# Two of four memory-value products moved to the experts' norm block, one behind a post norm's sums, with a reordered branches block, in an fp32 transformer kernel

## Chip, cores and metric

One NeuronCore of one Trainium2 chip runs the whole forward pass in one launch. The metric is the device time of one execution in microseconds (us), median of the runs shown. The profile is of one execution, whose span is counted from its first to its last instruction.

## What is computed

Three residual blocks over 256 tokens of width 1024, in fp32: feed-forward and gating layers, an attention block with a mixture of 32 experts, and a third block, which is the one that the change touches. Its part that matters here, cut:

```python
h = rms_norm_3(x, norm_mix_pre[l])
proj = h @ w_in[l]
q, k, v, u, gate_logits = jnp.split(proj, splits, axis=-1)
gate_attn, gate_ssm = jnp.split(jax.nn.sigmoid(gate_logits + b_gate[l]), 2, axis=-1)
o_attn = stick_breaking_attention(q, k, v)
o_ssm = s5_branch(u, ...)
merged = gate_attn * (o_attn @ w_branch_attn[l]) + gate_ssm * (o_ssm @ w_branch_ssm[l])
x = x + rms_norm_3(merged @ w_out[l], norm_mix_post[l])
h = rms_norm_3(x, norm_xa_pre[l])
mem_n = rms_norm_3(mem, norm_mem[l])
xa = memory_cross_attention(h, mem_n, xa_wq[l], xa_wk[l], xa_wv[l], xa_wo[l])
```

`memory_cross_attention` begins with `k = mem_n @ wk` and `v = mem_n @ wv`, both 256 x 1024 by 1024 x 1024. They depend on `mem` and weights alone, so they can be multiplied at any time before the cross attention. `s5_branch` ends with `y = gelu(y)` and `y * sigmoid(y @ w_glu + b_glu)`.

## The kernel before

The program is a row of blocks (`nc.Block`); in each, the five engines run their own streams, and all meet at its end, so that none begins the next block before the last is done. Within a block the order on an engine is the order of the code, and semaphores tie the engines. Weights pass through a ring of eight 1 MB slots in SBUF (`Ring`); a unit of weights is one slot, loaded by SyncE's queue once the slot's last reader is done. PSUM has eight banks, each with a full and a free semaphore (`Banks`).

The experts' stage (`run_items`) goes through (expert, token group) items. Each item uses slots 0 to 7 and four more for its expert's weights. Beside the items, `MemoryRows` normalizes and turns `mem` into the tile `memory`, done by item 17. After the last item comes the experts' norm block, `rmsnorm` (L320): ScalarE squares the expert sum, VectorE adds the squares, TensorE sums them over partitions with ones (L357), ScalarE takes the root (L346), VectorE inverts it (L374), scales (L382) and adds to the residual (L386). SyncE loads six units for the next block in it.

`two_branches` then runs `dense_up` (its first unit is L1089) for q, k, v and u, and after it the branches block, `branches` (L3642 on). In that block TensorE interleaves three things:

- the stick-breaking attention: scores (L3724), turned weights (L3737) and values (L3749). The logarithms and exponentials between them are ScalarE's (L3819 to L3826) and the suffix sums VectorE's (L3920 to L3924);
- the state-space scan in four steps: inputs (L3759), copies by ScalarE (L3858), the scan and its products by VectorE (L3941 to L3958), outputs (L3770), then skip sums (L3962), a gelu (L3888) and the GLU product (L3804);
- twenty "native" units (`Native`, `native.multiply`, L1118) that fill the gaps: four of keys, four of values, eight of gates and four of the attention branch. Keys are copied by ScalarE at L3837, values at L3842, gates pass a sigmoid (L3849), and branch units are gated by VectorE (L3973). They use three slots (unit n loads once unit n-3 is multiplied) and two banks in turn (unit n waits until unit n-2 is read).

SyncE's stream in this block is all twenty unit loads first, and then the load of the GLU weights (L3702), which only needs the attention values to be done. ScalarE copies the first keys after `log_fail(3)`, and the third key unit needs that bank.

Behind it come `dense_down` blocks: the state-space branch, the output projection with `PostNorm` (squares L654, sums L644 and L647, root L656, scaling L675, addition L681), the cross query (first unit L820), the cross attention, its projection, and the convolutional feed-forward. Each takes its slots from the ring in turn.

## Time and profile before

| | us |
|---|---|
| median of 3 runs (lowest, highest) | 2831.14 (2826.31, 2832.01) |
| the profiled execution's own time | 2825.68 |
| its span | 2823.9 |
| TensorE (PE) busy | 2648.1, 94% of the span |
| VectorE (DVE) busy | 1431.8, 51% |
| ScalarE (ACT) busy | 968.0, 34% |
| mean granted TensorE clock, of full speed | 0.967 |

The span's shares are averages over stages with different limits. The stage of the change lies between 2229 us (the norm block) and 2530 us (the block after the post norm). The trace records a fp32 matmul as two rows, so that a native unit of 16 matmuls (keys, values and gates) shows as x32, and a branch unit of 8 as x16. A row "PEq" as the releaser of an idle time is the meeting of the engines at a block's end. The clock column is the granted clock as a share of 2.4 GHz: 0.50 is 1.2 GHz.

### The profile page before, as it was taken

What the parts mean: (1) busy time and instruction counts of PE and PEld (TensorE: products, weight loads), DVE (VectorE), ACT (ScalarE), POOL (GpSimd) and SP (SyncE); (2) the same over time, 40 slices, a digit from 0 to 9 for tenths busy, and PEclk for the clock granted to TensorE, in tenths of its full rate; (3) what the DMA queues carried; (4) which work ended last, traced back from release to release, by engine and by line L of the source; (5) the groups of instructions that cost most, each with busy time, mean ns of one, the idle gap of its engine ahead of it and who ended that gap; (6) DMA issues with size and microseconds to landing.
All of it is one profiled execution on the core that took longest, in us unless ns stands there. A gap on an engine that the chain in (4) does not pass through costs nothing. (4 is left out here: it accounts for less than half of the span.)

```text
span 2823.9 us, 41236 instructions
## 1 busy us (share of the span) xinstructions
PE 2648.1 (94%) x16344; PEld 1958.3 (69%) x16345; DVE 1431.8 (51%) x1975; ACT 968.0 (34%) x1179; POOL 7.8 (0%) x15
## 2 busy tenths in 40 slices
PE   7999899999999989799999999999999789988998
PEld 6898788988998977654444444444444378777988
DVE  6846468577468647533244222222212457255893
ACT  4425446355346422421111211211212262123662
POOL 0000000000000000000000000000000000000000
PEclk9999999999999999889999999999999899999999
DMA  7664546657465631189979999999989534442452
GB/s 231 233 225 153 209 140 202 232 169 256 169 217 181 221 137 60 53 336 420 420 308 420 419 420 419 420 421 420 421 345 401 206 96 121 136 158 90 149 193 75
DMA packets 259034, 698.81 MB, mean 247 GB/s; under 512 B 18403, under 2 KB 177838, under 8 KB 209614
## 3 DMA queue, kind: packets, MB, share of 16 engines
q1 hardware_dynamic: 258452, 695.89, 64.8%
q8 instruction: 82, 1.34, 0.2%
q10 hardware_dynamic: 474, 1.37, 0.2%
q14 instruction: 26, 0.21, 0.0%
HBM read 696.16 MB, written 1.05 MB: 247 GB/s over the span
## 5 line engine op out<-in xcount | busy, mean ns | idle before, releaser
L854 DVE TENSOR_TENSOR weight_parts<-weight_slots,weight_parts 128x2048 fp32r<-128x2048 f32 x208 | 473.7, 2288 | 181.3 <-ACT weight_parts L848 179.4
L3093 PE MATMUL bank<-weight_slots,item_x 128*64 128x512 f32 x2176 | 495.8, 604 | 23.5 <-DMA weight_slots<-in_w_mlp 23.5
L848 ACT ACTIVATE weight_parts<-weight_slots 128x2048 fp32r<-128x2048 f32 x208 | 393.4, 1908 | 215.6 <-DMA weight_slots<-in_ffn_w_out 79.8
L1061 PE MATMUL bank<-h_parts,weight_parts 128*128 128x512 f32 x1536 | 384.1, 392 | 0.0
L3093 PEld LDWEIGHTS bank<-weight_slots,item_x 128*64 128x64 f32 x2176 | 151.8, 138 | 315.3 <-issue 287.7
L3268 DVE TENSOR_TENSOR expert_sum_then_keys<-bank,expert_sum_then_keys 128x512 f32<-128x512 f32 x136 | 84.5, 683 | 496.2 <-PE bank L3137 496.2
L866 PE MATMUL bank<-hidden_high,weight_parts 128*128 (+1 forms) x1760 | 314.5, 281 | 8.5 <-DVE weight_parts L854 8.5
L1061 PEld LDWEIGHTS bank<-h_parts,weight_parts 128*128 128x128 f32 x1536 | 275.0, 188 | 47.9
L866 PEld LDWEIGHTS bank<-hidden_high,weight_parts 128*128 128x128 f32 x1760 | 271.0, 189 | 9.5 <-issue 9.5
L3124 PE MATMUL bank<-weight_slots,item_act 128*64 128x512 f32 x1088 | 246.3, 606 | 6.6 <-DVE item_act L3261 3.2
L866 PE MATMUL bank<-hidden_low,weight_parts 128*128 (+1 forms) x880 | 246.6, 280 | 0.0
L1063 PEld LDWEIGHTS bank<-h_parts,weight_parts 128*128 128x128 f32 x1536 | 205.9, 188 | 15.9
L1063 PE MATMUL bank<-h_parts,weight_parts 128*128 128x256 f32 x1536 | 209.6, 278 | 0.0
L3124 PEld LDWEIGHTS bank<-weight_slots,item_act 128*64 128x64 f32 x1088 | 80.1, 141 | 171.0 <-issue 170.2
L3188 ACT ACTIVATE item_hidden<-bank 128x512 f32<-128x512 f32 x68 | 36.9, 595 | 431.0 <-PE bank L3093 431.0
L866 PEld LDWEIGHTS bank<-hidden_low,weight_parts 128*128 128x128 f32 x880 | 165.9, 189 | 0.0
L3080 PEld LDWEIGHTS bank<-item_select,tokens_then_values 128*128 128x128 f32 x1088 | 130.3, 196 | 29.7 <-issue 26.8
L3080 PE MATMUL bank<-item_select,tokens_then_values 128*128 128x64 f32 x1088 | 135.6, 279 | 2.5 <-DVE item_select L3235 2.5
L3202 ACT ACTIVATE item_y<-bank 128x512 f32<-128x512 f32 x34 | 20.3, 597 | 325.8 <-PE bank L3124 325.8
L3253 DVE TENSOR_TENSOR item_glu<-bank,b_columns 128x512 f32<-128x512 f32 x34 | 23.5, 692 | 206.2 <-PE bank L3106 206.2
L866 PE MATMUL bank<-h_parts,weight_parts 128*128 128x256 f32 x1008 | 120.6, 280 | 3.6 <-DVE weight_parts L854 3.6
L1409 ACT ACTIVATE low_sums<-bank 128x512 f32<-128x512 f32 x88 | 52.5, 597 | 206.4 <-PE bank L1063 206.4
(591 smaller groups left out, 3251.8 us busy)
## 6 DMA issues: line engine op xcount, KB each, us to landing
weight_slots<-in_w_mlp SPq DMA_DIRECT2D x384, 1024.0 KB, 17.4
weight_slots<-in_ffn_w_in SPq DMA_DIRECT2D x88, 1024.0 KB, 5.1
weight_slots<-in_ffn_w_out SPq DMA_DIRECT2D x44, 1024.0 KB, 7.3
weight_slots<-in_ffn_w_up SPq DMA_DIRECT2D x22, 1024.0 KB, 5.2
weight_slots<-in_a_w_in SPq DMA_DIRECT2D x16, 1024.0 KB, 6.8
weight_slots<-in_w_in SPq DMA_DIRECT2D x16, 1024.0 KB, 5.7
weight_slots<-in_ffn_w_down SPq DMA_DIRECT2D x11, 1024.0 KB, 7.2
weight_slots<-in_a_w_out SPq DMA_DIRECT2D x8, 1024.0 KB, 13.3
```

Source lines behind the costliest of these rows:

```text
L848: K.nc.scalar.activation(high, source, ACT.Copy).then_inc(K.high_written.sem, 1)
L854: K.nc.vector.tensor_tensor(low, place, high.bitcast(F32), ALU.subtract)\
L866: m = K.nc.tensor.matmul(out, stationary[a], moving[b], start=start and n == 0, stop=stop and n == 2, **flags)
L1061: K.nc.tensor.matmul(ps, high[k], flat(pair[:, k, :, :]), start=k == 0, stop=False, skip_group_check=True)
L1063: last = K.nc.tensor.matmul(ps[:, 0:S], low[k], pair[:, k, 0, :], start=False, stop=k == DT - 1, skip_group_check=True)
L1409: K.nc.scalar.activation(self.lows[:, b, g, :, :], K.banks.columns(ats, 1), ACT.Copy).then_inc(K.lows_copied.sem, 1)
L3080: m = nc.tensor.matmul(ps[(2, 7)[q]][:, t % 4 * CAP:(t % 4 + 1) * CAP], M.tokens[:, b, t * P:(t + 1) * P], sel[:, b, :], start=b == 0, sto ...
L3093: m = nc.tensor.matmul(ps[c // 2][half(c % 2), :], x[:, s, :], ring.slot(s)[:, c * 512:(c + 1) * 512], start=s == 0, stop=s == 7, skip_gro ...
L3124: m = nc.tensor.matmul(ps[3][half(c), :], act_t[:, turned_tile(t), :], ring.slot(s)[:, kk * D + c * 512:kk * D + (c + 1) * 512], start=t = ...
L3188: m = nc.scalar.activation(hid[:, b, :], ps[b][:, :], copy)
L3253: link(v.tensor_tensor(glu[:, :, :], ps[4][:, :].rearrange("p (t s) -> p t s", t=DT), bias(0), ALU.add))
L3268: v.tensor_tensor(part, ps[4 + j][:, :], part, ALU.add).then_inc(sem.added, 1)
```

## The change

Of the four value units, two (`late_values`, banks 4 and 5, ring slots 6 and 7) are loaded at the end of the experts' stage, behind SyncE's wait for the last item's use of their slot, and multiplied in the experts' norm block: the first half of unit 0 ahead of the sum matmuls, its second half and unit 1 behind them, and ScalarE's two copies behind the root. One (`value`, bank 4, the next ring slot) is loaded behind the output projection's weights and multiplied behind the post norm's sums, with its copy behind the root. The fourth stays a native unit. For this the tile `memory` lives until the post norm, and the first gates get a buffer of their own. All ring units taken after it move on by one slot.

In the branches block there are seventeen native units. SyncE loads units 0 to 7, then the GLU weights, then the rest. ScalarE copies the first keys ahead of `log_fail(3)`. One branch unit comes ahead of the last state outputs and is gated ahead of the skip sums, so between the last state outputs and the GLU product stands one branch unit where there were two gate and two branch units.

```diff
@@ -317,7 +317,7 @@
-def rmsnorm(K, src, dst, gain, tiles, shift=None, add_to=None, loads=None, modulation=None, room=None):
+def rmsnorm(K, src, dst, gain, tiles, shift=None, add_to=None, loads=None, modulation=None, room=None, beside=()):
@@ -347,10 +349,14 @@
                 modulation.read_rows(act)
+            for unit in beside:
+                unit.read(act)
...
+            for unit in beside[0:1]:
+                unit.multiply(pe, (0,))
             K.banks.vacant(pe, bank)
@@ -358,6 +364,8 @@
                 modulation.turn(pe)
+            for n, unit in enumerate(beside):
+                unit.multiply(pe, (0, 1) if n else (1,))
@@ -646,6 +654,8 @@
         m.then_inc(K.banks.full[6], 1)
+        if self.beside is not None:
+            self.beside.multiply(pe, (0, 1))
@@ -655,6 +665,8 @@
             .then_inc(K.banks.free[6], 1)
+        if self.beside is not None:
+            self.beside.read(act)
@@ -2980,8 +2992,9 @@
-        run_items(K, a, M, T, memory)
-        rmsnorm(K, M.sum[:, :, :], None, lambda t: K.gate2[:, t:t + 1], DT, add_to=K.x[:, :, :], loads=following.issue)
+        run_items(K, a, M, T, memory, values)
+        rmsnorm(K, M.sum[:, :, :], None, lambda t: K.gate2[:, t:t + 1], DT, add_to=K.x[:, :, :], loads=following.issue,
+                beside=values)
@@ -3070,6 +3083,10 @@
                     sp.dma_start(ring.slot(s), w2[bass.ds(e, 1), s - 8].rearrange("e p n -> p (e n)")).then_inc(loaded[s], 16)
+            n = number_of(sp)
+            for unit in values:
+                sp.wait_ge(used[unit.unit[0]], n)
+                unit.issue(sp)
@@ -3499,17 +3516,63 @@
+class MemoryValues:
+    def __init__(self, K, weights, mem, out, bank):
+        self.K, self.weights, self.mem, self.out, self.bank = K, weights, mem, out, bank
+        self.unit = K.ring.take()
+    def plan(self):
+        self.at = self.K.banks.take(self.bank)
+        self.K.ring.freed_by(self.unit[0], self.K.banks.full[self.bank], self.at[2] + 1)
+    def issue(self, sp):
+        K = self.K
+        K.ring.vacant(sp, self.unit)
+        sp.dma_start(K.ring.slot(self.unit[0]).rearrange("p (t n) -> p t n", n=256),
+                     self.weights.rearrange("(t p) n -> p t n", p=P)).then_inc(K.ring.loaded[self.unit[0]], 16)
+    def multiply(self, pe, blocks):
+        K, b = self.K, self.at[0]
+        slot = K.ring.slot(self.unit[0])
+        for block in blocks:
+            if block == 0:
+                K.banks.vacant(pe, self.at)
+                K.ring.arrived(pe, self.unit)
+            for k in range(DT):
+                m = K.nc.tensor.matmul(K.ps[b][:, block * 256:(block + 1) * 256], self.mem[:, k, block * P:(block + 1) * P],
+                                       slot[:, k * 256:(k + 1) * 256], start=k == 0, stop=k == DT - 1)
+            if block == 1:
+                m.then_inc(K.banks.full[b], 1)
+    def read(self, act):
+        K, b = self.K, self.at[0]
+        K.banks.ready(act, self.at)
+        K.nc.scalar.activation(self.out, K.ps[b][:, :].rearrange("p (b n) -> p b n", b=TB), ACT.Copy).then_inc(K.banks.free[b], 1)
+class Together:
+    def __init__(self, *parts):
+        self.parts = parts
+    def issue(self, sp):
+        for part in self.parts:
+            part.issue(sp)
...
-    def __init__(self, K, a, stack):
+    def __init__(self, K, a, stack, turned_rows):
...
-        self.K = K
+        self.K, self.turned_rows = K, turned_rows
...
-        self.turned_rows = stack.enter_context(nc.sbuf_tensor("memory", [P, DT, S], F32))
@@ -3597,14 +3660,16 @@
-        o = buffer("attention_out", 4, S)
-        gates = [memory.turned_rows[:, :, :], early[:, 4 * S:12 * S].rearrange("p (t s) -> p t s", s=S)]
+        o, first_gates = buffer("attention_out", 4, S), buffer("first_gates", DT, S)
+        gates = [first_gates[:, :, :], early[:, 4 * S:12 * S].rearrange("p (t s) -> p t s", s=S)]
...
-        dense_down(K, y, w_ssm, Gated(K, K.h, gates[1]), w_out)
-    return w_out
+        value = MemoryValues(K, a["xa_wv_3"][0][:, 2 * 256:3 * 256], memory.turned_rows, v_mem[:, :, 2 * 256:3 * 256], 4)
+        value.plan()
+        dense_down(K, y, w_ssm, Gated(K, K.h, gates[1]), Together(w_out, value))
+    return w_out, value
@@ -3683,7 +3748,7 @@
-    value_at = [native.add(a["xa_wv_3"][0][:, j * 256:(j + 1) * 256], mem, DT, True) for j in range(4)]
+    value_at = native.add(a["xa_wv_3"][0][:, 3 * 256:4 * 256], mem, DT, True)
@@ -3695,11 +3760,12 @@
         def _(sp):
-            native.load(sp)
+            native.load(sp, 0, 8)
             for at in turned_at[1]:
...
             sp.dma_start(glu, a["ssm_w_glu_3"][0].rearrange("(t p) n -> p t n", p=P)).then_inc(glu_loaded, 16)
+            native.load(sp, 8, len(native.units))
             w_ssm.issue(sp)
@@ -3792,8 +3858,7 @@
-            for n in range(14, 18):
-                native.multiply(pe, n)
+            native.multiply(pe, 14)
@@ -3804,8 +3869,8 @@
                 m.then_inc(banks.full[at[0]], 1)
-            native.multiply(pe, 18)
-            native.multiply(pe, 19)
+            native.multiply(pe, 15)
+            native.multiply(pe, 16)
@@ -3836,11 +3901,10 @@
-            def memory_values(j):
-                at = value_at[j]
-                banks.ready(act, at)
-                nc.scalar.activation(v_mem[:, :, j * 256:(j + 1) * 256], ps[at[0]][:, :].rearrange("p (b n) -> p b n", b=TB),
...
+            def memory_values():
+                banks.ready(act, value_at)
+                nc.scalar.activation(v_mem[:, :, 3 * 256:4 * 256], ps[value_at[0]][:, :].rearrange("p (b n) -> p b n", b=TB),
@@ -3863,8 +3927,8 @@
             exponentials(1)
+            keys(0)
             log_fail(3)
-            keys(0)
             exponentials(2)
@@ -3873,16 +3937,16 @@
-            memory_values(0)
-            memory_values(1)
+            memory_values()
+            gate(0)
...
-            memory_values(2)
-            memory_values(3)
+            gate(1)
+            gate(2)
...
-            gate(0)
-            gate(1)
+            gate(3)
+            gate(4)
...
-            for j in range(2, 8):
+            for j in range(5, 8):
@@ -3922,6 +3986,13 @@
+            def branch(j):
+                at = branch_at[j]
+                banks.ready(dve, at)
+                banks.read(dve, gate_at[j])
+                V.tensor_tensor(flat(K.h[:, 2 * j:2 * j + 2, :]), ps[at[0]][:, :], flat(gates[0][:, 2 * j:2 * j + 2, :]), ALU.mult)\
+                    .then_inc(banks.free[at[0]], 1)
@@ -3956,6 +4027,7 @@
                 V.tensor_tensor(im_cos, wim, c, ALU.mult).then_inc(products_written, 1)
+            branch(0)
             for n in range(Q):
@@ -3966,14 +4038,7 @@
-            def branch(j):
-                at = branch_at[j]
-                banks.ready(dve, at)
-                banks.read(dve, gate_at[j])
-                V.tensor_tensor(flat(K.h[:, 2 * j:2 * j + 2, :]), ps[at[0]][:, :], flat(gates[0][:, 2 * j:2 * j + 2, :]), ALU.mult)\
-                    .then_inc(banks.free[at[0]], 1)
-            for j in range(4):
+            for j in range(1, 4):
@@ -4146,14 +4211,17 @@
-            nc.sbuf_tensor("tokens_then_values", [P, TB, D], F32) as values:
+            nc.sbuf_tensor("tokens_then_values", [P, TB, D], F32) as values, nc.sbuf_tensor("memory", [P, DT, S], F32) as mem:
...
-            T, memory = S5Operands(K, a, stack), MemoryRows(K, a, stack)
+            T, memory = S5Operands(K, a, stack), MemoryRows(K, a, stack, mem)
+            K.ring.next, K.ring.limit = 6, SLOTS
+            late_values = [MemoryValues(K, a["xa_wv_3"][0][:, j * 256:(j + 1) * 256], mem, values[:, :, j * 256:(j + 1) * 256], 4 + j)
+                           for j in range(2)]
...
-            experts(K, a, T, memory, keys, values, branch_weights)
-            mixed_weights = two_branches(K, a, T, memory, keys, values, branch_weights)
-        up_weights = cross_attention(K, a, mixed_weights, keys, values, lambda: PairWeights(K, a["ffn_w_up_3"][0]))
+            experts(K, a, T, memory, keys, values, branch_weights, late_values)
+            mixed_weights, value = two_branches(K, a, T, memory, keys, values, branch_weights)
+        up_weights = cross_attention(K, a, mixed_weights, value, keys, values, lambda: PairWeights(K, a["ffn_w_up_3"][0]))
```

TensorE at the end of the experts' stage and in the norm block, before; the tile names are those of the sums of squares and the experts' weights:

```order
L3124 MATMUL bank<-weight_slots,item_act 64x512 x16
L3137 MATMUL bank<-item_gates_t,item_y 128x256 x8
L3043 UNCONDITIONAL_BRANCH
L351 UNCONDITIONAL_BRANCH
L357 MATMUL bank<-norm_squares,consts 128x256 x2
L330 UNCONDITIONAL_BRANCH
L956 UNCONDITIONAL_BRANCH
L1089 MATMUL bank<-h_normed,weight_slots 128x256 x8
```

and with the change:

```order
L3141 MATMUL bank<-weight_slots,item_act 64x512 x16
L3154 MATMUL bank<-item_gates_t,item_y 128x256 x8
L3056 UNCONDITIONAL_BRANCH
L355 UNCONDITIONAL_BRANCH
L3544 MATMUL bank<-weight_slots,memory 128x256 x8
L363 MATMUL bank<-norm_squares,consts 128x256 x2
L3544 MATMUL bank<-weight_slots,memory 128x256 x24
L332 UNCONDITIONAL_BRANCH
L968 UNCONDITIONAL_BRANCH
L1101 MATMUL bank<-h_normed,weight_slots 128x256 x8
```

L3544 is the value product; its first 8 matmuls stand ahead of the 2 sum matmuls, and 24 between those and the end of the block.

TensorE at the end of the branches block, before (L3770 state outputs, L3804 the GLU product, `attention_out` the branch units):

```order
L3759 MATMUL bank<-s_u,s_b 128x256 x8
L1118 MATMUL bank<-h_normed,weight_slots 128x256 x32
L3770 MATMUL bank<-weight_slots,s_c 32x256 x16
L1118 MATMUL bank<-h_normed,weight_slots 128x256 x32
L3770 MATMUL bank<-weight_slots,s_c 32x256 x16
L1118 MATMUL bank<-h_normed,weight_slots 128x256 x32
L1118 MATMUL bank<-attention_out,weight_slots 128x256 x16
L3804 MATMUL bank<-qkv_then_gates,spare 128x256 x16
L1118 MATMUL bank<-attention_out,weight_slots 128x256 x16
L3694 UNCONDITIONAL_BRANCH
```

and with the change (L3836 state outputs, L3869 the GLU product):

```order
L3825 MATMUL bank<-s_u,s_b 128x256 x8
L1130 MATMUL bank<-h_normed,weight_slots 128x256 x32
L3836 MATMUL bank<-weight_slots,s_c 32x256 x16
L1130 MATMUL bank<-h_normed,weight_slots 128x256 x16
L1130 MATMUL bank<-attention_out,weight_slots 128x256 x8
L3836 MATMUL bank<-weight_slots,s_c 32x256 x16
L1130 MATMUL bank<-attention_out,weight_slots 128x256 x8
L3869 MATMUL bank<-qkv_then_gates,spare 128x256 x16
L1130 MATMUL bank<-attention_out,weight_slots 128x256 x16
L3759 UNCONDITIONAL_BRANCH
```

Three units fewer stand in the block, 8 branch matmuls stand ahead of the last state outputs, and 8 between them and the GLU product in place of 48.

SyncE in the branches block, before:

```order
L3696 UNCONDITIONAL_BRANCH
L3631 DMA weight_slots<-in_xa_wk 128x8x256 x4
L3631 DMA weight_slots<-in_xa_wv 128x8x256 x4
L3631 DMA weight_slots<-in_w_in 128x8x256 x8
L3631 DMA weight_slots<-in_w_branch_attn 128x4x256 x4
L3702 DMA spare<-in_ssm_w_glu 128x4x512
L712 DMA weight_slots<-in_w_branch_ssm 128x2x1024 x2
L3694 UNCONDITIONAL_BRANCH
```

and with the change:

```order
L3761 UNCONDITIONAL_BRANCH
L3696 DMA weight_slots<-in_xa_wk 128x8x256 x4
L3696 DMA weight_slots<-in_xa_wv 128x8x256
L3696 DMA weight_slots<-in_w_in 128x8x256 x3
L3767 DMA spare<-in_ssm_w_glu 128x4x512
L3696 DMA weight_slots<-in_w_in 128x8x256 x5
L3696 DMA weight_slots<-in_w_branch_attn 128x4x256 x4
L724 DMA weight_slots<-in_w_branch_ssm 128x2x1024 x2
L3759 UNCONDITIONAL_BRANCH
```

The load into `spare` (the GLU weights) has moved ahead of five gate loads and all branch loads.

## Rows read from the trace of the kernel before

**Rows 1.** Page, part 1: busy time, share of the span, instructions.

```profile
PE 2648.1 (94%) x16344; PEld 1958.3 (69%) x16345; DVE 1431.8 (51%) x1975; ACT 968.0 (34%) x1179; POOL 7.8 (0%) x15
```

**Rows 2.** Timeline across the experts' end, the norm block and the next block's start (start us, us, engine, line).

```profile
2229.58 2.19 ACT L344 ACTIVATE norm_squares<-expert_sum_then_keys 128x512 f32<-128x512 f32 x4 [4.37 <-PEq L3043]
...
2233.05 2.05 PE L357 MATMUL bank<-norm_squares,consts 128*128 128x256 f32 x4 [5.79 <-DVE norm_squares L367]
...
2240.72 2.29 DVE L386 TENSOR_TENSOR x_residual<-x_residual,norm_squares 128x2048 f32<-128x2048 f32 x1
2243.29 2.19 ACT L488 ACTIVATE qkv_then_gates<-x_residual 128x512 f32<-128x512 f32 x4 [7.68 <-PEq L330]
...
2244.08 5.35 PE L1089 MATMUL bank<-h_normed,weight_slots 128*128 128x256 f32 x16 [8.98 <-DVE h_normed L494]
```

**Rows 3.** Windows: us, busy of PE, PEld, DVE, ACT, POOL, granted clock, DMA.

```profile
2227.30:2230.00 2.70, 0.00 (x0) 0.00 (x0) 1.63 (x3) 0.42 (x1) 0.00 (x0) 1.00 0.00 0
2230.00:2233.00 3.00, 0.00 (x0) 0.00 (x0) 2.08 (x3) 2.98 (x5) 0.00 (x0) 0.56 0.59 147
...
2301.00:2304.00 3.00, 2.86 (x9) 2.42 (x10) 1.81 (x4) 2.97 (x4) 0.00 (x0) 0.68 1.10 349
2519.30:2523.00 3.70, 3.67 (x9) 2.98 (x10) 3.63 (x10) 3.70 (x5) 0.00 (x0) 0.50 0.82 313
```

**Rows 4.** TensorE's timeline, the branches block from its first key on.

```profile
2301.14 15.74 PE L1118 MATMUL bank<-memory,weight_slots 128*128 128x256 f32 x64 [2.25 <-DMA weight_slots<-in_xa_wk]
...
2320.46 7.17 PE L1118 MATMUL bank<-memory,weight_slots 128*128 128x256 f32 x32 [2.71 <-ACT expert_sum_then_keys L3837]
...
2341.32 14.08 PE L1118 MATMUL bank<-weight_slots,memory 128*128 128x256 f32 x64
...
2420.20 1.93 PE L3770 MATMUL bank<-weight_slots,s_c 128*32 128x256 f32 x32
...
2446.43 10.03 PE L3804 MATMUL bank<-qkv_then_gates,spare 128*128 128x256 f32 x32 [3.38 <-DMA spare<-in_ssm_w_glu]
2456.29 7.07 PE L1118 MATMUL bank<-attention_out,weight_slots 128*128 128x256 f32 x32
2465.85 8.83 PE L820 MATMUL bank<-qkv_then_gates,weight_slots 128*128 128x256 f32 x32 [2.49 <-PEq L3694]
```

**Rows 5.** ScalarE's timeline in the branches block.

```profile
2315.33 1.04 ACT L3819 ACTIVATE weight_slots<-weight_slots 128x1024 f32<-128x1024 f32 x1
...
2319.83 0.58 ACT L3837 ACTIVATE expert_sum_then_keys<-bank 128x512 f32<-128x512 f32 x1
...
2437.03 1.28 ACT L3888 ACT_TABLE_LOAD   x1
2438.33 1.06 ACT L3888 ACTIVATE qkv_then_gates<-qkv_then_gates 128x1024 f32<-128x1024 f32 x1
```

**Rows 6.** VectorE's timeline: the state chain's first and last instruction, the skip sums.

```profile
2343.83 1.22 DVE L3941 TENSOR_TENSOR weight_slots<-weight_slots,s_angle 128x1024 f32<-128x1024 f32 x1 [3.68 <-ACT weight_slots L3859]
...
2411.59 1.22 DVE L3958 TENSOR_TENSOR weight_slots<-weight_slots 128x1024 f32<-128x1024 f32 x1
...
2422.20 0.87 DVE L3962 SCALAR_TENSOR_TENSOR qkv_then_gates<-s_u,params,bank 128x256 f32<-128x256 f32 x2 [8.61 <-PE bank L3770]
```

**Rows 7.** SyncE's timeline: the transfer of the GLU weights.

```profile
2440.18 0.37 SPq L3702 DMA_DIRECT2D spare<-in_ssm_w_glu  x1
```

**Rows 8.** Page, part 6: one weight transfer of 1 MB (last figure: us to landing).

```profile
weight_slots<-in_ffn_w_up SPq DMA_DIRECT2D x22, 1024.0 KB, 5.2
```

**Rows 9.** Timelines of TensorE and VectorE around the post norm.

```profile
2509.28 1.03 PE L647 MATMUL bank<-late_squares,consts 128*128 128x256 f32 x4
...
2516.98 1.28 DVE L681 TENSOR_TENSOR x_residual<-x_residual,late_squares 128x512 f32<-128x512 f32 x2
```

**Rows 10.** Timeline, the block behind the post norm.

```profile
2519.33 9.41 PE L820 MATMUL bank<-h_normed,weight_slots 128*128 128x256 f32 x32 [9.03 <-DVE h_normed L494]
```

20 lines of the change are left out of this document (11 added, 9 removed).

## The prediction

> **What bounds the kernel now.** I began with the busy shares: TensorE works 94% of the span [rows 1], so the change can only pay where TensorE's work moves into its idle time, or where idle time of its own goes. Next I read the timeline around the norm block [rows 2]. TensorE's sum matmuls (L357) start at 2233.05 after 5.79 us idle, so its experts' work ended at 2227.26. They run 2.05 us to 2235.10, and then it stands still for 8.98 us until 2244.08. What ends that block is the chain behind the sums: root, inverse, scaling, addition, the last ending at 2240.72 + 2.29 = 2243.01. Then the branches block [rows 4]: there TensorE's row is almost unbroken, and its few gaps name their releasers: 2.71 us for ScalarE's copy of the first keys, and 3.38 us for the GLU weights. Last, the post norm: sums end at 2509.28 + 1.03 = 2510.31 [rows 9], and TensorE waits 9.03 us for the next block's operand [rows 10]. So there are two holes of 9 us, and between them a full block (2301 to 2463 us in rows 4) in which TensorE is the bound.
>
> The price of a unit: 64 rows take 14.08 us [rows 4], so a unit of 32 rows is 7.04 us at 2.4 GHz, half of one 3.52, and a branch unit 3.52.
>
> **Branches block.** Removed: three value units, 3 x 7.04 = 21.1 us, all on TensorE's unbroken row.
>
> The first keys' copy. ScalarE is done with its exponentials at 2315.33 [rows 5] and copies at 2319.83, after `log_fail(3)`. The first two keys end at 2301.14 + 15.74 = 2316.88 [rows 4], the first of them well before 2315.33. Copied ahead of `log_fail(3)`, the bank is free when TensorE has turned the first weights, and the 2.71 us go. The cost is 0.58 us of ScalarE [rows 5] ahead of the last logarithm, and the last quarter's exponentials come 0.6 us later; TensorE asks for them only behind the third key unit (7.17 us, rows 4) and the first attention values, so I cost it at nothing. If that cover is short, it is at most 0.6.
>
> The GLU weights. SyncE issues them at 2440.18 [rows 7], last but for two, since each unit's load ahead of them waits for a slot. With the change they are issued once unit 4 is multiplied, about 2346, and land some 70 us before use. The wait of 3.38 us goes. So does what it brings: the GLU product takes 10.03 us, where 32 rows at 2.4 GHz take 7.07 [rows 4], for the clock falls in the wait: 3.0 us. The gate loads are now behind SyncE's wait for the attention values; those are done near 2337, before unit 4, so the queue is held by nothing new.
>
> Does something else end the block? VectorE's state chain runs without a break from 2343.83 to 2411.59 + 1.22 = 2412.81 [rows 6]. It starts 2.7 us sooner, so its last products are there at 2410.1. TensorE's last state outputs now start at 2420.20 [rows 4]. With the change the same number of native units stands before them, but one is a branch unit: 2420.20 - 2.7 - 3.5 = 2414.0. So TensorE remains the bound by 3.9 us. Behind them the skip sums (0.87), a sync copy and the gelu (1.06) must be done before the GLU product [rows 5, 6]: about 2.2 us, against 3.52 us of the one branch unit that is left as cover (before, there were 21 us). If the 1.28 us table load [rows 5] doesn't run ahead, that is 3.5 against 3.5: nothing, at most 1.3. I take nothing.
>
> Sum: 21.1 + 2.7 + 3.4 + 3.0 = 30.2 us saved; bounds 28.3 and 30.2.
>
> **Norm block.** Added: 64 rows of value product. The weights come in time: their slots are freed by the last item's first product, which ends before the 2227 us at which the experts' work does, by more than its second product; a transfer of 1 MB takes 5.2 us to land [rows 8]. SyncE has nothing else to issue there.
>
> The block opens at 2229.58 [rows 2]. At a block where TensorE's work was ready (L820) it stood idle 2.49 us [rows 4], so here it starts at 2227.26 + 2.49 = 2229.75. The half unit is 3.52 at full clock, ending at 2233.3, next to the 2233.05 at which the squares are there. But the granted clock is 1.00 up to 2230 and 0.56 after it [rows 3]: 1.2 GHz. Of the rows behind a short idle, L820's 32 rows took 8.83 instead of 7.07 [rows 4], 1.8 more. I take that: the half ends at 2235.0. The four sum rows then go at 2.4 GHz in 1.03 [rows 9] and not 2.05, and end at 2236.1, 1.0 later than now. The remaining 48 rows take 10.56, to 2246.6, and ScalarE's last copy 0.6, to 2247.3. VectorE's tail, 1.0 late, ends at 2244.0, so TensorE's work is what ends the block: 4.3 us later.
>
> Given back: the next block's first 16 rows now take 5.35 us at 1.2 GHz [rows 2], against 3.52. TensorE would have stood 1.8 us before them (0.28 to open, 0.8 to the operand, the rest the copy). After 2.25 and 2.49 us of idle the clock fell [rows 3, 4], after 2.71 us it did not (32 rows in 7.17). I take half of the 1.8: 0.9. Norm block: +4.3 - 0.9 = +3.4; bounds +0.8 (clock never low: 1.8 off at each end) and +4.3.
>
> The granted clock in this stretch is thus what decides the term. The Trainium skill, page "TensorE: Matmul & The Clock Gate", section "What's actually happening", says that the activity monitor runs free of the kernel, so how many matmuls run at the low level varies from run to run. By that rule either end of the bounds can come in either run, and the sum would be 25.9 or 29.4 in place of 26.8 for these two blocks; the unequal outcomes behind 2.49 and 2.71 us of idle agree with it.
>
> **Post norm.** Added: 32 rows, from 2510.31 to 2517.4, and the copy to 2518.0. VectorE's last addition ends at 2516.98 + 1.28 = 2518.26 [rows 9], so they are hidden, by 0.3 us only. The clock was 0.50 in the block behind it [rows 3], and its first 32 rows took 9.41 [rows 10]. With TensorE busy until 1.9 us before them, they take between 7.04 and 8.83: 0.6 to 2.4 less, and I take 1.5. The transfer (5.2 us, rows 8) is issued some 50 us earlier, behind four others.
>
> **Sum.** -30.2 + 3.4 - 1.5 = **-28.3 us**. The profiled execution took 2825.68, 5.5 below the median of the runs, 2831.14. Against the median the time is **2803 us**.
>
> **The rivals.**
>
> *The three halves run at 1.2 GHz.* In the trace the clock is 0.56 over 2230 to 2233 [rows 3], and the next block's first rows are slow still [rows 2]. If it does not come back in the norm block, 48 rows take 21.1 in place of 10.56, and the sum is -28.3 + 10.6 = -17.7: 2813. Against it: TensorE has no pause there, and each busy stretch in rows 4 came back to 2.4 GHz. 8%.
>
> *The state chain or the gelu takes over.* If ScalarE's sigmoids (now ahead of the second state inputs) or the single covering unit make VectorE late by more than its 3.9 us, part of the saving is given back. At 6 us, -22: 2809. For it: the cover of the gelu falls from 21 us to 3.5. Against it: ScalarE is idle through most of the block. 10%.
>
> *The units are not covered, only moved.* If TensorE is held in both holes (the reads of the bank or the meeting at the end wait for the units in full), 21.1 us come back and only the stalls are saved: -9.1, 2822. Against it: 9 us idle, measured, at both. 7%.
>
> *The ring moves on by one slot, and the time gets longer.* Every unit of weights behind the branches block sits in another slot. If a load there now waits for a slot whose reader is later, it is exposed: 22 transfers for the up projection [rows 8] and 11 for the down projection follow. From 0.86 us each this eats the 28.3; at 1.5 us each it is +49.5, which gives 2852. For it: the fourth unit of the query's weights really waits for the output projection's first unit. Against it: all the ring turns together, so each unit's distance from its slot's last reader stays, and that one load has over 25 us. 3%.
>
> **Chances.** The forecast 72%, the rivals 8, 10, 7 and 3%. Runs of this kernel spread from 2826.31 to 2832.01, and some 0.2% (5.7 us) is what a measurement can tell from no change. All cases but the last are faster by more; I leave 2% for something between. So faster 95%, the same 2%, slower 3%. The range: low, the lowest run less the best bounds (-30.2 + 0.8 - 2.4 = -31.8): 2794.5; high, up to between the first two rivals, 2812, which leaves out the first, third and fourth rival, 18%. I give 2793 to 2812.
>
> **What would show it.** Right: in the norm block, 16 value rows, 4 sum rows within 1.5 us, and 48 value rows without a gap, with the block's end at a ScalarE copy; the next block's first 16 rows near 3.6 to 5.3 us. In the branches block no gap at the third key unit and none at the GLU product, with its 32 rows in 7.1; VectorE's products ready 4 us before the last state outputs. Behind the post norm sums 32 rows, and the next opening not later. Wrong: a new wait named DMA at the value rows, a gap before the last state outputs or the GLU product, or longer gaps in the feed-forward.

## The result, and the profile after

| | before | after |
|---|---|---|
| median, 4 runs each | 2829.18 us | 2793.82 us |
| lowest to highest | 2826.31 to 2832.01 | 2792.38 to 2796.84 |
| ratio to before, 95% interval | | 0.9886 [0.9872, 0.9899] |
| profiled execution: its time, its span | 2825.68, 2823.9 | 2792.38, 2790.6 |

The kernel is 35.4 us faster by the medians and 33.3 us by the two profiled spans; 28.3 were forecast. The table cuts both profiles at the first instruction of each block (ScalarE's first square, or SyncE's first transfer of the block's weights), so each column is the time from one block's opening to the next one's. The "ssm projection" is the `dense_down` block of the state-space branch:

| us | experts | norm block | block behind it (L1101) | branches | ssm projection | output projection with post norm | from there to the end |
|---|---|---|---|---|---|---|---|
| before | 1039.68 | 13.71 | 52.51 | 169.75 | 16.60 | 36.36 | 305.39 |
| after | 1040.75 | 16.00 | 51.01 | 139.72 | 16.60 | 36.35 | 302.45 |
| difference | +1.1 | +2.3 | -1.5 | -30.0 | 0 | 0 | -2.9 |

Ahead of the experts the profile of after is another 2.2 us shorter; the change touches nothing there. Line numbers in this section are those of the changed kernel; the rows of an experiment have that kernel's own.

The norm block and the next one's opening, TensorE's timeline of after (start, us, engine, line, operation, operands, [idle before and its releaser]); it answers to [rows 2]:

```profile
2228.64 3.69 PE L3544 MATMUL bank<-weight_slots,memory 128*128 128x256 f32 x16 [2.48 <-PEq L3056]
2232.16 1.03 PE L363 MATMUL bank<-norm_squares,consts 128*128 128x256 f32 x4
2233.03 10.52 PE L3544 MATMUL bank<-weight_slots,memory 128*128 128x256 f32 x48
2245.26 3.69 PE L1101 MATMUL bank<-h_normed,weight_slots 128*128 128x256 f32 x16 [1.71 <-DVE h_normed L502]
```

The three pieces stand where the prediction put them: 16 value rows (the first half of unit 0, called the head half below), four sum rows at 1.03 us, 48 rows without a gap. The first hole of 5.79 us is down to 2.48 and the one of 8.98 to 1.71, and all of it runs at 2.4 GHz: the 16 rows at L1101 take 3.69 us, against 5.35. ScalarE and VectorE at the block's end:

```profile
2236.68 0.60 ACT L3552 ACTIVATE tokens_then_values<-bank 128x512 f32<-128x512 f32 x1 [2.98 <-PE bank L3544]
2243.59 0.60 ACT L3552 ACTIVATE tokens_then_values<-bank 128x512 f32<-128x512 f32 x1 [6.31 <-PE bank L3544]
```

```profile
2238.82 2.29 DVE L394 TENSOR_TENSOR x_residual<-x_residual,norm_squares 128x2048 f32<-128x2048 f32 x1
```

VectorE, which ended the block before, is done at 2241.11. ScalarE's copy of the second unit ends it now, at 2244.19, behind TensorE's last value rows.

The branches block, TensorE's timeline of after; it answers to [rows 4]:

```profile
2300.75 14.05 PE L1130 MATMUL bank<-memory,weight_slots 128*128 128x256 f32 x64 [0.50 <-DMA weight_slots<-in_xa_wk]
2314.92 1.18 PE L3803 MATMUL bank<-consts,weight_slots 128*128 128x128 f32 x8
2315.93 7.16 PE L1130 MATMUL bank<-memory,weight_slots 128*128 128x256 f32 x32
2323.80 1.09 PE L3815 MATMUL bank<-weight_slots,qkv_then_gates 128*64 128x128 f32 x16 [0.71 <-ACT weight_slots L3896]
...
2413.62 1.93 PE L3836 MATMUL bank<-weight_slots,s_c 128*32 128x256 f32 x32
2415.49 3.72 PE L1130 MATMUL bank<-attention_out,weight_slots 128*128 128x256 f32 x16
2419.05 7.07 PE L3869 MATMUL bank<-qkv_then_gates,spare 128*128 128x256 f32 x32
2425.95 7.07 PE L1130 MATMUL bank<-attention_out,weight_slots 128*128 128x256 f32 x32
2435.51 8.83 PE L832 MATMUL bank<-qkv_then_gates,weight_slots 128*128 128x256 f32 x32 [2.49 <-PEq L3759]
```

No bracket stands at the third key unit (2315.93) nor at the GLU product (2419.05), which takes 7.07 us for 10.03. The rest is seen on VectorE, SyncE and ScalarE ([rows 5 to 7] before):

```profile
2408.44 1.22 DVE L4029 TENSOR_TENSOR weight_slots<-weight_slots 128x1024 f32<-128x1024 f32 x1
...
2415.63 0.87 DVE L4034 SCALAR_TENSOR_TENSOR qkv_then_gates<-s_u,params,bank 128x256 f32<-128x256 f32 x2 [0.43 <-PE bank L3836]
```

```profile
2345.97 0.44 SPq L3767 DMA_DIRECT2D spare<-in_ssm_w_glu  x1
```

```profile
2416.72 1.06 ACT L3952 ACTIVATE qkv_then_gates<-qkv_then_gates 128x1024 f32<-128x1024 f32 x1 [4.30 <-DVE exponential_sums L4039]
```

The state chain ends at 2409.66, 4.0 us ahead of the last state outputs at 2413.62. The gelu ends at 2417.78, 1.3 us ahead of the GLU product. The GLU transfer is issued at 2345.97, 73 us ahead of its use.

The post norm, TensorE's timeline of after; it answers to [rows 9, 10]:

```profile
2478.92 1.03 PE L655 MATMUL bank<-late_squares,consts 128*128 128x256 f32 x4
2479.78 7.07 PE L3544 MATMUL bank<-weight_slots,memory 128*128 128x256 f32 x32
2488.97 7.14 PE L832 MATMUL bank<-h_normed,weight_slots 128*128 128x256 f32 x32 [2.12 <-DVE h_normed L502]
```

The unit's 7.07 us lie wholly in the old hole of 9.03, and the 32 rows behind it take 7.14 us, for 9.41. Not every profile shows that gain whole: with the same unit and the same idle time these rows took 8.83 us in five of nine profiles (below).

### The profile page after: what moved, and what is told of

It reads as the page before. It is cut to its first block and busy times, and to the rows that moved or that the text cites. A ratio compares the mean times of both kernels' runs of the same rounds, so it can differ in the third digit from the quotient of the medians.

```text
span 2790.6 us, 41227 instructions
## 1 busy us (share of the span) xinstructions
PE 2637.9 (95%) x16344; PEld 1951.3 (70%) x16345; DVE 1431.4 (51%) x1975; ACT 967.9 (35%) x1179; POOL 7.8 (0%) x15
## 5 line engine op out<-in xcount | busy, mean ns | idle before, releaser
L3097 PEld LDWEIGHTS bank<-item_select,tokens_then_values 128*128 128x128 f32 x1088 | 130.3, 196 | 29.7 <-issue 26.8
```

The lines of the kernel that those rows point to most:

```text
L3097: m = nc.tensor.matmul(ps[(2, 7)[q]][:, t % 4 * CAP:(t % 4 + 1) * CAP], M.tokens[:, b, t * P:(t + 1) * P], sel[:, b, :], start=b == 0, sto ...
```

## The experiments

Two theories were set against each other for each term: the one of the prediction (TensorE's work moved into its idle time, two stalls gone) and, place by place, the rival that the gain is really another edit's, or that the clock or VectorE's chain takes it back. The twelve experiments ran in three groups with their own runs of before, whose medians were 2826.17, 2826.42 and 2828.04 us. Ratios are to those, with the 95% interval in brackets. The block times in the text are cut as in the table above.

### The stalls, one at a time

**The GLU transfer alone, in before** (SyncE's order of the change):

```
-            native.load(sp)
+            native.load(sp, 0, 8)
...
             sp.dma_start(glu, ...)
+            native.load(sp, 8, len(native.units))
```

> The kernel before, with only SyncE's order in the branches block changed: unit loads 0 to 7, the GLU weights, then the other twelve loads. Theory of the sum: the 3.4 us gap ahead of the GLU product goes, and its 32 rows take 7.07 in place of 10.03, 6.4 us in all, with nothing else moved; 0.9978 of before. Rival, the gap moves: the later unit loads, now behind the wait for the attention values, come late, a DMA gap shows at a gate unit, and less than 3 us are left of the gain.

2818.33 us, 0.9967 [0.9955, 0.9980]. The branches block takes 163.24 us for 169.75, so 6.5 us went. TensorE's timeline of this kernel:

```profile
2436.09 7.07 PE L1118 MATMUL bank<-attention_out,weight_slots 128*128 128x256 f32 x32
2443.00 7.07 PE L3805 MATMUL bank<-qkv_then_gates,spare 128*128 128x256 f32 x32
```

No wait and no slow rows are left. The slow rows were the wait's doing: with it gone, the same 32 rows take 7.07. The rival (the wait moves to a gate unit) did not come: no row of that kind names a transfer.

**The first keys' copy alone, in before** (`keys(0)` ahead of `log_fail(3)`):

> The kernel before, with only the first keys' copy ahead of the last logarithms. Theory of the sum: the gap of 2.7 us ahead of the third key unit goes and the branches block is 2.7 us shorter. Rival, ScalarE is the bound in this stretch: the gap comes back in pieces at the attention values and the second turn, as two gaps of 0.7 and 0.4 us in the changed kernel suggest, and 1.5 us or less are left.

2820.86 us, 0.9979 [0.9969, 0.9989]. The branches block is 2.3 us shorter (167.48). From the block's opening to the first state inputs (L3759 here) it is 41.89 us, 44.45 before and 41.65 in the changed kernel: 2.6 of the 2.7 forecast. TensorE's timeline shows what was not forecast:

```profile
2321.91 1.17 PE L3737 MATMUL bank<-consts,weight_slots 128*128 128x128 f32 x8 [0.33 <-ACT weight_slots L3826]
2322.92 7.17 PE L1118 MATMUL bank<-memory,weight_slots 128*128 128x256 f32 x32
2330.80 1.09 PE L3749 MATMUL bank<-weight_slots,qkv_then_gates 128*64 128x128 f32 x16 [0.71 <-ACT weight_slots L3831]
2333.34 1.09 PE L3737 MATMUL bank<-consts,weight_slots 128*128 128x128 f32 x8 [0.43 <-ACT weight_slots L3826]
```

ScalarE is late by 0.7 and 0.4 us in two places further on, in this kernel and in the changed one (and by 0.3 ahead of the first turned weights here). There the first two key units ran in 14.05 us for 15.74, so TensorE came sooner. Where they ran slow with the same early copy, as in the next experiment, no wait for ScalarE is left:

```profile
2301.41 15.74 PE L1130 MATMUL bank<-memory,weight_slots 128*128 128x256 f32 x64 [2.19 <-DMA weight_slots<-in_xa_wk]
```

and the stretch up to the first state inputs is 41.41 us, 3.0 below before. So the copy is worth its 2.6 to 3.0 us at either clock.

The two edits give 8.8 us of the 9.1 that the prediction gave them (2.7 + 3.4 + 3.0) by the blocks. The medians are further apart, 7.8 us for the first and 5.3 for the second, and for the second the whole interval (3.1 to 8.8 us) lies above the 2.3 of its block; its profiled execution was the slowest of ten (2830.39). Where the rest comes from was not followed.

### What a unit is worth in each place

**Two units back in the branches block** (the change without `beside` in the norm block; 19 native units, the third value unit still behind the post norm). One gate and two branch units now stand between the last state outputs and the GLU product, and all four branch units are gated behind the skip sums. Cut:

```
-            late_values = [MemoryValues(...) for j in range(2)]
+            late_values = []
...
-    value_at = native.add(... 3 * 256:4 * 256 ...)
+    value_at = {j: native.add(...) for j in (0, 1, 3)}
```

> The changed kernel with the two units of the norm block back among the native units (19 native units, one unit behind the post norm). Theory of the sum: 14.1 us more in the branches block; in exchange the norm block ends 2.3 sooner, and the next block's first rows are slow again, 1.5 to 1.8 longer; so 13.3 us above the changed kernel. Rival, the two units cost more in the norm block than the one profile shows (1.2 GHz in other executions, as the forecast had it with 4.3 and 0.9): then the difference of the medians is nearer 10.

2808.01 us, 0.9932 [0.9915, 0.9948]. Norm block 13.72, block behind it 52.62, branches 153.31: against the profile of the change -2.3, +1.6 and +13.6. Two units cost 13.6 there (14.1 forecast) and 0.7 net at the norm block, 2.4 where the head half ran slow. The 12.9 us between these agree with the two ratios (0.9932 and 0.9886, 13 us). The first 32 rows behind the post norm are at 7.14 us here too; since five other profiles with that unit show 8.83, this one alone does not tell what the two moved units do to them.

**The third unit back** (two in the norm block, units 2 and 3 native, nothing behind the post norm; two branch units between the last state outputs and the GLU product). Cut:

```
-        value = MemoryValues(K, a["xa_wv_3"][0][:, 2 * 256:3 * 256], ...)
-        dense_down(K, y, w_ssm, Gated(...), Together(w_out, value))
+        dense_down(K, y, w_ssm, Gated(...), w_out)
```

> The changed kernel with the third value unit back among the native units (two in the norm block, none behind the post norm, 18 native units). Theory of the sum: 7.0 us more in the branches block and 2.3 more behind the post norm, so 9.3 above the changed kernel, 24.6 below before. Rival, the unit behind the post norm is held off by its copy or the meeting at the end: then the post norm block is shorter here by a us or more, and the difference is 7 or less.

2807.74 us, 0.9933 [0.9917, 0.9950]. Branches 146.84, 7.1 above the change; the 32 rows behind the post norm 9.69 us, 2.5 above. But my edit brought a fault of its own, which TensorE's timeline names:

```profile
2446.10 9.43 PE L832 MATMUL bank<-qkv_then_gates,weight_slots 128*128 128x256 f32 x32 [4.99 <-DMA weight_slots<-in_w_branch_ssm]
```

With 18 native units the next block's weights go into the slot of the last of them and come late: 3.1 us in the ssm projection (19.71 for 16.60). Another 1.7 us is the norm block's first half, slowed by the clock (below). The third unit is thus worth 7.1 + 2.5 = 9.6 us by the blocks (9.3 forecast), and 0.9 + 7.1 = 8.0 where the rows behind it run at 8.83, not the 14 between the medians.

**A fourth unit in the norm block** (bank 7, its weights loaded into the first one's slot behind the branch weights; 16 native units):

```
     for unit in beside:
         unit.plan()
+    if beside:
+        late = MemoryValues(K, ..., mem, ..., 7)
+        late.plan()
+        beside = [*beside, late]
```

> The changed kernel with the fourth value unit in the norm block too (bank 7, slot 6 loaded again once unit 0 is multiplied), 16 native units. Theory: both places are now spent. TensorE ends the norm block, so the unit costs its full 7.0 us there, and more if its load, which stands behind six others in the queue, lands late (up to 6 more). In the branches block VectorE's state chain, which has 3.9 us of slack, becomes the bound: 7.0 us of work leave it and only 4 to 5 us come off, with a gap ahead of the last state outputs. In all 2 to 9 us slower than the changed kernel. Rival: the slack is not used up, 7.0 off against 7.0 on, and the time is equal.

2812.57 us, 0.9949 [0.9932, 0.9966]: 17.8 us above the change run again beside it, where 2 to 9 were expected: a miss. The norm block takes 34.69 us for 17.69. SyncE's timeline, then TensorE's:

```profile
2229.99 13.04 SPq L909 DMA_DIRECT2D weight_slots<-in_w_in  x6
2243.07 2.92 SPq L3542 DMA_DIRECT2D weight_slots<-in_xa_wv  x1
```

```profile
2236.26 10.52 PE L3553 MATMUL bank<-weight_slots,memory 128*128 128x256 f32 x48
2254.90 8.88 PE L3553 MATMUL bank<-weight_slots,memory 128*128 128x256 f32 x32 [8.11 <-DMA weight_slots<-in_xa_wv]
...
2431.24 2.48 PE L3844 MATMUL bank<-weight_slots,s_c 128*32 128x256 f32 x32 [2.96 <-DVE weight_slots L4033]
```

The load waits its turn behind six of 1 MB on SyncE's queue, and TensorE waits 8.11 us for it. (An estimate from these rows: its slot is free near 2236.26 + 3.5 = 2239.8, and with the 5.2 us of [rows 8] it could have landed by 2245.0, ahead of the end of the 48 rows at 2246.8.) The rows of the unit itself (8.88) are exposed whole, for this hole is full. And the branches block got only 1.1 us shorter (138.73) by a unit of 7.0. Now the state chain ends last, with 2.96 us of waiting for VectorE: a unit less than in the change uses up the 4.0 us that the chain had to spare. Behind that wait rows are slow for another 1.7 us (the state outputs 2.48 for 1.93, 16 branch rows 4.82 for 3.72), and up to the first state inputs the block is 1.25 us longer (42.90 for 41.65), with 2.01 us of waiting for the first key weights. The change stops at the right number.

### The two covers left in the branches block

**Both branch units ahead of the last state outputs** (nothing between these and the GLU product):

```
                 native.multiply(pe, 7 + 2 * n)
+                if n == 3:
+                    native.multiply(pe, 14)
                 state_outputs(n)
...
-            native.multiply(pe, 14)
             pe.wait_ge(glu_loaded, 16)
```

> The changed kernel with the second branch unit also ahead of the last state outputs, so that nothing stands between these and the GLU product. Theory: skip sums, sync copy and gelu are then open, a gap of 2.3 us (in the changed kernel the gelu ends 2.3 us after the last state outputs), and the clock may fall behind it, up to 1.8 more: the branches block is 2.3 to 4.1 us longer. Rival: the skip sums of the first two tiles and the table load are what takes long, the gap is 3.5 or more; or TensorE's work is the same and there is no difference.

2799.66 us, 0.9902 [0.9885, 0.9919]; branches 142.74, 2.9 above the change run beside it. TensorE's timeline:

```profile
2419.23 1.93 PE L3836 MATMUL bank<-weight_slots,s_c 128*32 128x256 f32 x32
2423.48 7.14 PE L3870 MATMUL bank<-qkv_then_gates,spare 128*128 128x256 f32 x32 [2.32 <-issue]
```

Without cover, skip sums and gelu show as 2.32 us, where the prediction worked out "about 2.2 us". The 3.52 us of one unit cover that, and the change loses nothing there. The table load runs ahead: it starts at 2411.14 in the profile of the change, 5.6 us before the gelu. The medians are 4.9 us apart; in this profile the rows behind the post norm took 8.83 us for 7.14, another 1.7.

### The norm block's head

**All 64 rows behind the sums** (no half unit ahead):

```
-            for unit in beside[0:1]:
-                unit.multiply(pe, (0,))
...
-                unit.multiply(pe, (0, 1) if n else (1,))
+                unit.multiply(pe, (0, 1))
```

> The changed kernel with no product ahead of the norm's sums: both units, 64 rows, stand behind them. Theory: TensorE ends the norm block, so the half unit that stood in the first hole is added behind, 3.5 us; the sums come 0.9 sooner without it only if they do not run at 1.2 GHz behind 5 us of idle, and they do (2.05 in place of 1.03). So the norm block is 3.3 to 3.7 us longer. Rival: the first half delays the sums by as much as it takes out behind them, and the times are equal.

2799.73 us, 0.9900 [0.9881, 0.9918]. The norm block takes 21.55 us. TensorE's timeline:

```profile
2232.10 2.05 PE L361 MATMUL bank<-norm_squares,consts 128*128 128x256 f32 x4 [5.78 <-DVE norm_squares L373]
2233.94 15.32 PE L3542 MATMUL bank<-weight_slots,memory 128*128 128x256 f32 x64
2250.96 3.69 PE L1099 MATMUL bank<-h_normed,weight_slots 128*128 128x256 f32 x16 [1.71 <-DVE h_normed L500]
```

The old hole of 5.78 us is back, the sums take 2.05 again, and the first of the 64 rows are slow too (15.32, not 14.08). That is 5.55 us above the profile of the change, and 3.86 above those in which the head half itself was slow (17.69, next), where 3.3 to 3.7 were expected. The head is what makes the block cheap, at either clock.

**The change again, unchanged:**

> The changed kernel once more, beside the others of this group. Theory of the sum: the stages of the change give 33 us against the kernel before, 0.988 of it; by stage: norm block and the one behind it +0.8 where the first half runs at 2.4 GHz and +2.5 where it runs at 1.2, branches block -30.0, the block behind the post norm -0.6 or -2.3 by its clock. Rival, part of the 35.4 us of the medians came from the experts' stage and the feed-forward, whose clocks vary from run to run: then it is 31 to 33 here.

2794.81 us, 0.9880 [0.9864, 0.9897], which is 33.2 us below its own before (35.4 the first time). In the norm block its profile differs from the first one in one row (TensorE's timeline):

```profile
2233.91 5.38 PE L3544 MATMUL bank<-weight_slots,memory 128*128 128x256 f32 x16 [2.48 <-PEq L3056]
2239.13 1.03 PE L363 MATMUL bank<-norm_squares,consts 128*128 128x256 f32 x4
2239.99 10.52 PE L3544 MATMUL bank<-weight_slots,memory 128*128 128x256 f32 x48
2252.22 3.69 PE L1101 MATMUL bank<-h_normed,weight_slots 128*128 128x256 f32 x16 [1.71 <-DVE h_normed L502]
```

Same program, same 2.48 us idle, and the head half takes 5.38 us for 3.69: the block 17.69 for 16.00. The profiled span is 6.8 us longer than the first one (2797.4 and 2790.6); 5.3 of that lie ahead of the norm block, where both executions run the same code. The granted clock over the head half, in z_after and in the first profile of the change (columns: window, us, busy and count per engine, granted clock, DMA share, GB/s):

```profile
2233.90:2239.10 5.20, 5.19 (x16) 4.27 (x17) 2.08 (x3) 3.31 (x5) 0.00 (x0) 0.67 0.79 235
```

```profile
2228.70:2232.10 3.40, 3.40 (x16) 3.01 (x17) 2.08 (x3) 3.24 (x5) 0.00 (x0) 1.00 0.69 170
```

A stretch of the first one is at 1.2 GHz; the other is at 2.4 throughout.

### The clock behind the post norm, and a faster version

**Constant matmuls in the post norm's hole, in before** (16 whose result nobody reads):

```
         m.then_inc(K.banks.full[6], 1)
+        for n in range(16):
+            f = K.nc.tensor.matmul(K.ps[4][:, ...], K.ones, K.consts[:, 0:S], start=True, stop=True)
```

> The kernel before, with 16 extra matmuls of two constant tiles (32 rows, no result is used) behind the post norm's sums, in the hole of 9 us; no value unit is moved. Theory: TensorE's activity ahead of the opening is what gave the extra time behind the post norm. The next block's first 32 rows take 7.1 in place of 9.4 and the time falls by 2.3 us, although no work was removed. Rival: the gain there came with the moved unit or its ring slot; then the rows stay at 8.8 or more and the time is equal.

2827.40 us, 1.0003 [0.9993, 1.0013]: a miss. TensorE's timeline:

```profile
2509.61 7.07 PE L654 MATMUL bank<-consts 128*128 128x256 f32 x32
2518.81 8.83 PE L827 MATMUL bank<-h_normed,weight_slots 128*128 128x256 f32 x32 [2.13 <-DVE h_normed L494]
```

The same 7.07 us of work, the same 2.13 us idle behind it, and the 32 rows take 8.83, not 7.14: 0.6 won. A busy TensorE ahead of the opening is not enough to say which of the two it will be. Since rows behind a real value unit took 8.83 as well in five profiles, this one profile does not show that the unit's gain needs the unit.

**Half a unit earlier still** (the first unit's first half in the last item's tail in bank 2, while TensorE waits there for VectorE; its second half as head; only the second unit behind the sums):

```
             turn_gates(n)
+            values[0].multiply(pe, (0,))
             second_product(n, ...)
...
             for unit in beside[0:1]:
-                unit.multiply(pe, (0,))
+                unit.multiply(pe, (1,))
```

> The changed kernel with the first half of unit 0 one step sooner: in the last item's tail, where TensorE waits 3.2 us for the activations, in bank 2; the second half ahead of the norm's sums, unit 1 behind them. Theory: TensorE is 3.1 us over VectorE's tail in the norm block, and with 16 rows less there VectorE ends it, 3.1 us sooner; in the item's tail 16 rows take 3.5 in a hole of 3.2 and keep the clock up, so the second product there takes about 7.1 to 8.5 in place of 8.5 to 9.7. In all 3 to 4.5 us below the changed kernel. Rival: the weights are not there yet (the load is issued at 2207, 5 us to land, the hole opens at 2211.7), TensorE waits for DMA in the tail, and what is won in the norm block is paid there.

2790.14 us, 0.9868 [0.9848, 0.9889]. TensorE's timeline:

```profile
2212.23 3.69 PE L3546 MATMUL bank<-weight_slots,memory 128*128 128x256 f32 x16 [0.69 <-DMA weight_slots<-in_xa_wv]
2215.86 7.09 PE L3142 MATMUL bank<-weight_slots,item_act 128*64 128x512 f32 x32
...
2227.97 3.69 PE L3546 MATMUL bank<-weight_slots,memory 128*128 128x256 f32 x16 [2.34 <-PEq L3057]
2231.50 1.03 PE L363 MATMUL bank<-norm_squares,consts 128*128 128x256 f32 x4
2232.37 7.07 PE L3546 MATMUL bank<-weight_slots,memory 128*128 128x256 f32 x32
```

In the change, run beside the later version, that product stands behind 3.24 us of waiting for `item_act`, and takes 10.05:

```profile
2218.68 10.05 PE L3141 MATMUL bank<-weight_slots,item_act 128*64 128x512 f32 x32 [3.24 <-DVE item_act L3278]
```

The norm block is down to 13.57 us, and VectorE's addition ends it again. By the ratios the version is 3 to 5 us below the two runs of the change, as expected (3 to 4.5), but the intervals overlap.

**The same, with the constant matmuls in the two other post norms** (mixed attention's and the cross attention's):

> As the one before, and 16 matmuls of two constant tiles (no result is used) behind the sums of two other post norms, those ahead of the experts and ahead of the feed-forward of the last block. Theory: each of the two blocks behind them opens at 2.4 GHz, 2.3 us less each if TensorE is the bound there, so 4 to 5 us below the one before. Rival: the extra rows or their waits show as a longer post norm, or the blocks behind start bound by another engine, and there is no gain.

2788.50 us, 0.9854 [0.9833, 0.9876]: 1.6 us below the version without them, where 4 to 5 were expected, a miss. The 9.03 us hole at the feed-forward's opening is 2.1 us, and that block 109.8 us for the 111.6 of the version without them.

**Again, beside the change:**

> The version with a half unit in the last item's tail and constant matmuls behind two other post norms, again. Theory: 2.4 us off the norm block, 1 to 1.6 off the item's tail, 1.5 to 2.3 off the block behind the post norm that now is warmed ahead of the feed-forward; 5 to 6 us below the changed kernel of this group. Rival, the terms are below what varies: within 3 us of it.

2786.80 us (2783.00 to 2795.92), 0.9865 [0.9847, 0.9884], where the change has 2794.81 (2792.65 to 2799.21). TensorE's timeline of it and of the change, at the expert router behind mixed attention's post norm:

```profile
1189.51 2.25 PE L2760 MATMUL bank<-router_w,h_normed 128*128 128x32 f32 x16 [2.12 <-DVE h_normed L2899]
```

```profile
1192.52 3.59 PE L2753 MATMUL bank<-router_w,h_normed 128*128 128x32 f32 x16 [9.03 <-DVE h_normed L2892]
```

The fastest version found: 8.0 us below the change by the medians. The intervals of the ratios overlap, and runs of this version spread over 12.9 us, so the order of these two is likely, not settled. What the constant matmuls give is not shown. In this second profile the 16 rows at the feed-forward's opening took 5.38 us behind 2.12 of idle (3.69 in the first), and the block 111.3. The two profiled executions are 16.2 us apart; 7.9 of it lie between the router's rows and the norm block, of which the last item's tail accounts for 1.7, and that stretch varies from 1038.5 to 1042.5 us among the eleven profiles with neither edit.

## Why the prediction was right

The result, 2793.82 us, lies in the range (2793 to 2812) at its lower edge, and on the forecast side. The mechanism came as forecast. That the number is inside is in part luck: the prediction's own best sum, 31.8 us off the lowest run, gave 2794.5, and the result is 0.7 below that, inside only since the range was rounded out to 2793. Both clocks that the sum left open fell near their good ends in the first profile, and the rest came from the spread of the runs. Step by step:

- **Branches block, -30.2 forecast, -30.0 measured.** Units: 13.6 for two and 7.1 for the third, 20.7 for 21.1. Both stalls together 8.8 for 9.1. That adds up to 29.5; the 0.5 us left over were not followed further. ScalarE's 0.58 us ahead of the last logarithm, "I cost it at nothing", were nothing where the key units ran slow; where they ran at 2.4 GHz they show as waits of 0.7 and 0.4 us, and the stretch is shorter than before all the same.
- **Covers.** The state chain's slack was 3.9 forecast and is 4.0; the gelu's wait 2.2 forecast and is 2.32 without cover. Both were worked out by adding up rows of three engines, and both decided how far the change could go: the fourth unit runs into the first.
- **Norm block with the next opening, +3.4 forecast; +0.8 in the first profile, +2.5 in the second.** This is the term that was mis-sized. The head half ran at 2.4 GHz in the profile that was compared (3.69 for the 5.3 taken) and in part at 1.2 in the second (5.38); in that one the block is +4.0, beside the 4.3 forecast. What was given back at the next opening, "I take half of the 1.8: 0.9", was the whole each time: -1.5 us by the blocks. All nine profiles with value rows ahead of that opening show its 16 rows in 3.69 us, behind 1.7 to 2.9 us of idle. The bounds (+0.8 to +4.3) held both. The sentence on the Trainium skill's page "TensorE: Matmul & The Clock Gate", section "What's actually happening", which says that the number of matmuls at the low level varies from run to run, fits: one program showed 3.69 and 5.38 in two executions. What it would do to the time was given as "25.9 or 29.4 in place of 26.8" for the two blocks; the profiles have 29.2 and, with the second one's branches block (139.87), 27.4.
- **Post norm, -1.5 forecast, -2.3 in both profiles of the change.** Only the clock was open. With the unit and the same 2.12 us of idle it came out at 7.14 us in four of nine profiles and at 8.83 in five, so -2.3 or -0.6: the bounds of the prediction, and both profiles of the change at the good one is luck. The unit is hidden as said: ScalarE's copy ends at 2487.49, VectorE's addition at 2487.90.
- **The base.** The sum was made against the profiled time, 5.5 us below the three runs' median, and put on that median. The spans differ by 33.3, of which 30.0 - 0.8 + 2.3 = 31.5 are the change's steps (29.7 by the second profile of the change, with its 29.9, 2.5 and 2.3); 1.1 (experts: +1.1, ahead of them: -2.2) and 0.6 at the end belong to stages whose work the change leaves as it was. The other 2.1 us up to 35.4 are where the two profiled executions stand in their own spread (3.5 and 1.4 below their medians).

The rivals. *Three halves at 1.2 GHz*: the 48 rows ran in 10.52 us in all five profiles that have them. *Only moved*: two units back in the branches block cost 12.9 us net by the blocks, so they are covered. *State chain or gelu*: not in the change, but one step away from it. *The ring moved on*: in the feed-forward behind the change the only waits for transfers are ScalarE's, and they are the same before and after (waits from the cross attention's end on: us in total, times, longest):

```profile
ACT weight_parts L848 <- DMA weight_slots<-in_ffn_w_down: 19.3, 4, 8.5
```

```profile
ACT weight_parts L860 <- DMA weight_slots<-in_ffn_w_down: 19.6, 4, 8.5
```

Its two large parts take 110.6 and 106.2 us for 111.3 and 106.2.

## What to carry to other kernels

Where one engine bounds a block and another block has that engine idle behind a reduction, move whole independent units there, and split one so that its first half fills the gap ahead of the reduction: the half unit ahead was worth 3.9 to 5.6 us, more than its own 3.5. Before each further unit, count the slack of the chain that becomes the bound (4.0 us here, and one more unit used it up) and look at the queue that its weights come by (the load behind six others cost 8.1 us). A transfer that needs no slot of the ring need not queue behind loads that do: that order was worth 6.5 us here, nearly half of it because the rows behind the wait had run slow too.

## What the runs showed of the hardware that I had not expected

- The same idle gap is followed by either clock, in one and the same program too. Behind 2.34 to 2.49 us of idle the head half took 3.69 us in three profiles and 5.38 in five; behind 2.12 us, with a busy TensorE before, the 32 rows of the post norm's next block took 7.14 us in four and 8.83 in six. Behind 1.71 to 2.87 us at L1101 no profile showed a slow row. So a term that hangs on the clock behind such a gap needs both values, and one profile does not decide it.
- Filling an idle hole with work that nobody needs gave next to nothing: the constant matmuls behind the post norm turned 9.03 us of idle into 2.13 and won 0.6 us in the profile, nothing in the median. The 2.13 us that stayed were enough for slow rows behind them.
